# Query and key projection with high and low parts side by side, and ScalarE writing 40 pairs of convolution tap products

## The reference, cut to what matters

```python
h = rmsnorm(x, pre_norm_g) * (1.0 + scale) + shift
proj = h @ w_in
q, k, v, z_ret, u_val, u_gate, z_conv, g_a, g_b = split(proj)
qh = rotary(q); kh = rotary(k) * 256 ** -0.5             # 4 heads of 256
ret = head_groupnorm(retention_chunkwise(qh, kh, v))
y_a = (ret * silu(z_ret)) @ w_ret_out
a = u_val * sigmoid(u_gate)
a = causal_depthwise_conv_2(a, conv_w, conv_b)           # 31 taps, 1024 channels
a = silu(layernorm(a, conv_ln_g, conv_ln_b))
y_b = (a * silu(z_conv)) @ w_conv_out
y = (sigmoid(g_a) * y_a + sigmoid(g_b) * y_b) @ w_out
```

## Time and profile before

| | |
|---|---|
| median of 3 runs | 837.8 us (837.55 to 839.03) |
| the profiled execution | 837.87 us, of which the span of the trace is 836.1 us |
| TensorE busy | 827.8 us, 99% |
| VectorE busy | 731.1 us, 87% |
| ScalarE busy | 500.2 us, 60% |
| granted TensorE clock | 0.999 of full speed |

### The profile page before, as it was taken

The page is one execution under the profiler, slowest core; times in us unless marked ns, Lnnn a source line. Parts: engine busy times, 40 slices in busy tenths (PEclk is TensorE's granted clock), DMA queues, the critical chain, the costliest instruction groups (busy, mean ns, idle before and its releaser), DMA issues.

```text
span 836.1 us, 13942 instructions
## 1 busy us (share of the span) xinstructions
PE 827.8 (99%) x5146; PEld 725.1 (87%) x5146; DVE 731.1 (87%) x1179; ACT 500.2 (60%) x804; POOL 45.4 (5%) x46
## 2 busy tenths in 40 slices
PE   8999999999999999999999999999999999999997
PEld 8999998789888888888888788998887798888886
DVE  7799899868877898888989979999999999988774
ACT  6899858576566555555565775333346675546743
POOL 0001101341100000000000000000001220000000
PEclk9999999999999999999999999999999999999999
DMA  9875675511875877777776656655454435564531
GB/s 277 256 253 169 211 245 174 146 38 45 278 232 179 261 262 263 257 256 252 238 257 218 221 185 213 202 184 169 155 198 151 152 118 200 186 231 171 188 115 50
DMA packets 129882, 164.13 MB, mean 196 GB/s; under 512 B 17407, under 2 KB 92199, under 8 KB 129703
## 3 DMA queue, kind: packets, MB, share of 16 engines
q1 hardware_dynamic: 129831, 163.45, 59.9%
HBM read 159.20 MB, written 4.23 MB: 195 GB/s over the span
## 4 chain that ended last, share of the span: by engine, by line
PE 98%; DVE 1%; DMA 1%; issue 0%; ACT 0%; DVEq 0%; SPq 0%; ACTq 0%
PE psum L695 16%; PE psum L727 14%; PE psum L728 14%; PE psum L734 14%; PE psum L704 8%; PE psum L677 6%; PE psum L686 6%; PE psum L678 6%; PE psum L1028 2%; PE psum L631 1%; PE psum L641 1%; PE psum L635 1%; PE psum L1033 1%; PE psum L915 1%; PE psum L1146 1%; PE psum L1134 1%
## 5 line engine op out<-in xcount | busy, mean ns | idle before, releaser
L1220 ACT ACTIVATE w_hi<-w_raw 128x1024 fp32r<-128x1024 f32 x255 | 266.6, 1061 | 188.2 <-PE psum L734 87.1
L1786 DVE TENSOR_TENSOR w_lo<-w_raw,w_hi 128x1024 fp32r<-128x1024 f32 x256 | 305.2, 1221 | 44.3 <-ACT w_hi L1220 42.2
L695 PE MATMUL psum<-hT,w_hi 128*128 128x512 f32 x576 | 138.9, 391 | 0.0
L695 PEld LDWEIGHTS psum<-hT,w_hi 128*128 128x128 f32 x576 | 105.4, 188 | 20.2
L727 PE MATMUL psum<-w_hi,hT 128*128 128x512 f32 x280 | 113.3, 405 | 0.0
L728 PE MATMUL psum<-w_hi,hT 128*128 128x512 f32 x280 | 109.3, 390 | 0.0
L2399 DVE SCALAR_TENSOR_TENSOR cv<-aP,par,cv 128x256 f32<-128x256 f32 x240 | 107.9, 519 | 0.0
L677 PE MATMUL psum<-hT,w_hi 128*128 128x256 f32 x432 | 107.4, 286 | 0.0
L678 PE MATMUL psum<-hT,w_hi 128*128 128x256 f32 x432 | 105.9, 283 | 0.0
L677 PEld LDWEIGHTS psum<-hT,w_hi 128*128 128x128 f32 x432 | 82.8, 192 | 0.4 <-issue 0.2
L678 PEld LDWEIGHTS psum<-hT,w_hi 128*128 128x128 f32 x432 | 82.9, 192 | 0.3 <-issue 0.2
(11 more groups left out here) (341 smaller groups left out, 1108.6 us busy)
## 6 DMA issues: line engine op xcount, KB each, us to landing
w_raw<-in_w_in_dram SPq DMA_DIRECT2D x44, 1024.0 KB, 5.1
w_raw<-in_sc_w_in_dram SPq DMA_DIRECT2D x32, 1024.0 KB, 7.9
w_raw<-in_gdn_w_in_dram SPq DMA_DIRECT2D x23, 1024.0 KB, 7.1
ada<-in_w_ada_dram SPq DMA_DIRECT2D x24, 512.0 KB, 4.8
w_raw<-in_gdn_w_out_dram SPq DMA_DIRECT2D x8, 1024.0 KB, 5.5
w_raw<-in_sc_w_out_dram SPq DMA_DIRECT2D x8, 1024.0 KB, 6.4
w_raw<-in_w_ret_out_dram SPq DMA_DIRECT2D x8, 1024.0 KB, 5.1
w_raw<-in_w_conv_out_dram SPq DMA_DIRECT2D x4, 1024.0 KB, 5.1
```

The lines of the kernel that those rows point to most:

```text
L695: pe.matmul(o, w_hi[s][:, k, mine], hT[:, h * KH2 + k, :, :], start=h == 0 and k == 0, stop=False, skip_group_check=True)
L1220: act.activation((w_hi[half_slot(g, h)] if home is None else third_hi[half_slot(g, home)])[:, :, :], raw[slot][:, h * KH2:(h + 1) * KH2, : ...
L1786: return dve.tensor_tensor(o, whole, hi.bitcast(F32), ALU.subtract)
```

## The change

TensorE: qk uses `chunk_apart`, still in a hardware loop, and the scores of v's chunk 0 wait for a doubled count of `rp_step`. ScalarE: in each step of qk it copies the low parts' share from PSUM to SBUF (`glu_part`). In qk, v and zret it also writes products of a window and a tap's weight for a pair of channel blocks (`make_taps`, two ACTIVATE of 128 x 256 for each of the 40 pairs), ahead of the phase's own work; there are two buffers at a time, so that each pair waits for the addition of the one before the last. VectorE: `rotate` first adds the two shares (`ug_sum`) and multiplies that sum; of the convolution 80 operations L2399 go and 40 additions of 128 x 512 come. The shares are now 1 addition in each chunk of qk, 4 operations and 2 additions in each of v and zret (chunk 2 of zret, where a pair of blocks ends, has 6 and 2), 8, 5, 5, 5 in zconv, 6, then five times 10, then 1 in gates. Each operation waits by `tap_before` for the last one on its own block. Waits of other engines on `cv_step` follow the new counts, and ScalarE's phases qk and v are unrolled.

```diff
+CONV_SHARES = [("glu", [(0, 0), (0, 0), (3, 0), (4, 0), (5, 0), (4, 0), (2, 0), (4, 0)]), ("qk", [(0, 1)] * 8), ("v", [(4, 2)] * 8),
+               ("zret", [(4, 2)] * 8), ("zconv", [(8, 0), (5, 0), (5, 0), (5, 0)]), ("gates", [(6, 0)] + [(10, 0)] * 7)]
+TAP_PHASES = ("qk", "v", "zret")
+
+
+def conv_order():
+    order, ends, part = [], [], {}
+    pair, tap, e = 0, 0, 0
+    for name, counts in CONV_SHARES:
+        for c, (singles, made) in enumerate(counts):
+            mine = part[name, c] = []
+            while (singles or made) and pair < KT // 2:
+                if singles or e or tap == 0:
+                    mine.append(("one", pair, tap, e))
+                    tap, e, singles = tap + e, 1 - e, max(singles - 1, 0)
+                else:
+                    mine.append(("made", pair, tap, None))
+                    tap, made = tap + 1, made - 1
+                order.append(mine[-1])
+                if tap == CW:
+                    ends.append(len(order))
+                    pair, tap = pair + 1, 0
+    assert pair == KT // 2
+    return order, ends, part
...
+def tap_before(i):
+    kind, pair, tap, e = CONV[i]
+    return max(j for j in range(i) if CONV[j][1] == pair and (e is None or CONV[j][3] in (None, e))) + 1
...
+        made = [at(f"made{s}", o_yT + 2 * s * K, [P, 2, SEQ]) for s in range(2)] + [at(f"made{s}", o_ada + 2 * (s - 2) * K, [P, 2, SEQ]) for s in (2, 3)]
+
+        def made_in(k):
+            first = sum(len([entry for entry in CONV_PART[name, c] if entry[0] == "made"])
+                        for name, cs in (("qk", range(COUNT["qk"])), ("v", range(4))) for c in cs)
+            return made[k % 2 + 2 * (k >= first)]
...
-                        elif name in ("sc_in", "glu"):
+                        elif name in ("sc_in", "glu", "qk"):
...
-                    pe.wait_ge(rp_step, 2 * RH)
+                    pe.wait_ge(rp_step, 4 * RH)
...
+            def make_taps(name, c):
+                for entry in CONV_PART[name, c]:
+                    kind, pair, tap, _ = entry
+                    if kind != "made":
+                        continue
+                    k = MADE.index(entry)
+                    act.wait_ge(bank_free, 4 + FIRST["qk"])
+                    if k >= 2:
+                        act.wait_ge(cv_step, CONV.index(MADE[k - 2]) + 1)
+                    if made_in(k) is not made[0] and made_in(k) is not made[1]:
+                        act.wait_ge(st_ready, RH)
+                    for e in range(2):
+                        n = 2 * pair + e
+                        w = par[:, 2 + tap // 16, tap % 16 * KT + n:tap % 16 * KT + n + 1]
+                        i = act.activation(made_in(k)[:, e, :], aP[:, n, tap:tap + SEQ], ACT.Copy, scale=w)
+                    i.then_inc(tap_made, 1)
...
-            chunks("qk")
+
+            def beside_qk_2(i, j, done):
+                c, g = 4 * i + j, FIRST["qk"]
+                make_taps("qk", c)
+                act.wait_ge(half_done, done)
+                act.wait_ge(bank_free, 4 + g + c - 1)
+                act.activation(glu_part[j % 2][:, :, :], psum[:, 2 * j:2 * j + 2, SEQ:2 * SEQ], ACT.Copy).then_inc(sc_act, 1)
+            chunks("qk", beside_qk_2, unroll=True)
...
-            chunks("v", tokens_out(vt, ACT.Copy))
+            v_out = tokens_out(vt, ACT.Copy)
+
+            def beside_v(i, j, done):
+                make_taps("v", 4 * i + j)
+                v_out(i, j, done)
+            chunks("v", beside_v, unroll=True)
...
+                make_taps("zret", c)
...
+                if kind == "made":
+                    k = MADE.index(CONV[i])
+                    dve.wait_ge(tap_made, k + 1)
+                    dve.tensor_tensor(cv[:, both, :], cv[:, both, :], made_in(k)[:, :, :], ALU.add).then_inc(cv_step, 1)
+                    return
...
-                    dve.wait_ge(cv_step, step - 1)
...
-                conv_share(3)
+                conv_share("qk", c)
                 dve.wait_ge(half_done, done)
-                dve.tensor_tensor(rp1[:, :, :], bank(j), cos2, ALU.mult)
-                dve.tensor_tensor(rp2[:, :, :], bank(j), sin2, ALU.mult).then_inc(bank_free, 1)
+                dve.wait_ge(sc_act, 6 * KT - 2 + COUNT["glu"] - 2 + c + 1)
+                dve.tensor_tensor(ug_sum[:, :, :], psum[:, 2 * j:2 * j + 2, 0:SEQ], glu_part[j % 2][:, :, :], ALU.add).then_inc(bank_free, 1)
                 dve.wait_ge(bank_free, 4 + FIRST["qk"] + c + 1)
+                dve.tensor_tensor(rp1[:, :, :], ug_sum[:, :, :], cos2, ALU.mult)
+                dve.tensor_tensor(rp2[:, :, :], ug_sum[:, :, :], sin2, ALU.mult).then_inc(rp_step, 1)
+                dve.wait_ge(rp_step, 2 * c + 1)
                 dve.tensor_tensor(qkT[:, 2 * c:2 * c + 1, :], rp1[:, 0:1, :], rp2[:, 1:2, :], ALU.subtract)
                 dve.tensor_tensor(qkT[:, 2 * c + 1:2 * c + 2, :], rp2[:, 0:1, :], rp1[:, 1:2, :], ALU.add).then_inc(rp_step, 1)
-                dve.wait_ge(rp_step, c + 1)
+                dve.wait_ge(rp_step, 2 * c + 2)
...
-                conv_share(9 if c < RH else 8)
+                conv_share("v", c)
...
-                conv_share(7)
+                conv_share("zret", n)
...
-                conv_share(5 if j else 8)
+                conv_share("zconv", j)
...
-                conv_share(10 if c else 4)
+                conv_share("gates", c)
```

More of the change, by code:

```diff
@@ L93 @@
 SHIFTED = ((4, 5, 6, 7), (6, 7))
+CONV_SHARES = [("glu", [(0, 0), (0, 0), (3, 0), (4, 0), (5, 0), (4, 0), (2, 0), (4, 0)]), ("qk", [(0, 1)] * 8), ("v", [(4, 2)] * 8),
[20 more added lines that the diff above has]
+    return order, ends, part
+CONV, CONV_ENDS, CONV_PART = conv_order()
+MADE = [entry for entry in CONV if entry[0] == "made"]
+def tap_before(i):
+    kind, pair, tap, e = CONV[i]
+    return max(j for j in range(i) if CONV[j][1] == pair and (e is None or CONV[j][3] in (None, e))) + 1
 E_LEAST = 0.5 * math.log(RMS_EPS) - 0.1
@@ L281, in build @@
         ba_hi_ready, ba_lo_ready, ba_done = sem("ba_hi_ready"), sem("ba_lo_ready"), sem("ba_done")
-        beta_ready, gate_v, gate_a, g_ready = (
-            sem(n) for n in ("beta_ready", "gate_v", "gate_a", "g_ready"))
+        tap_made, gate_v, gate_a, g_ready = (
+            sem(n) for n in ("tap_made", "gate_v", "gate_a", "g_ready"))
         bg_turned, bgt_ready, eg_ready = sem("bg_turned"), sem("bgt_ready"), sem("eg_ready")
@@ L1468, in _ @@
                     act.wait_ge(cleared, 1)
-                    act.activation(bg[0:VH, :], psum[0:VH, 6, 0:SEQ], ACT.Sigmoid).then_inc(beta_ready, 1)
+                    act.activation(bg[0:VH, :], psum[0:VH, 6, 0:SEQ], ACT.Sigmoid)
                     act.activation(acols[gr, 2:3], acols[gr, 0:1], ACT.Exp).then_inc(gate_a, 1)
@@ L1775, in _ @@
             pool.wait_ge(rg_ready, NT * RH)
-            pool.wait_ge(cv_step, CW * 4)
+            pool.wait_ge(cv_step, CONV_ENDS[1])
             pool.tensor_tensor(ln_sum[0][:, :, :], cv[:, 0:2, :], cv[:, 2:4, :], ALU.add).then_inc(ln_sum_step, 1)
             pool.wait_ge(ln_sum_step, 1)
-            pool.wait_ge(cv_step, CW * 6)
+            pool.wait_ge(cv_step, CONV_ENDS[2])
             pool.tensor_tensor(ln_sum[0][:, :, :], ln_sum[0][:, :, :], cv[:, 4:6, :], ALU.add).then_inc(ln_sum_step, 1)
@@ L2387, in _, with conv_op @@
             dve.memset(aP[:, :, 0:CPAD], 0.0).then_inc(padded, 1)
-            def conv_op(pair, tap, e):
-                n, step = 2 * pair + e, 2 * CW * pair + 2 * tap + e
+            conv_done = [0]
+            def conv_op(i):
+                kind, pair, tap, e = CONV[i]
+                both = slice(2 * pair, 2 * pair + 2)
+                if tap == 0 and e == 0:
+                    dve.wait_ge(bank_free, 4 + FIRST["glu"] + 2 * pair + 2)
+                if tap:
+                    dve.wait_ge(cv_step, tap_before(i))
+                if kind == "made":
[3 more added lines that the diff above has]
+                    return
+                n = 2 * pair + e
                 w = par[:, 2 + tap // 16, tap % 16 * KT + n:tap % 16 * KT + n + 1]
                 src = aP[:, n, tap:tap + SEQ]
-                if tap == 0 and e == 0:
-                    dve.wait_ge(bank_free, 4 + FIRST["glu"] + 2 * pair + 2)
                 if tap == 0:
@@ L2397, in conv_op, with conv_share @@
                 else:
-                    dve.wait_ge(cv_step, step - 1)
                     dve.scalar_tensor_tensor(out=cv[:, n, :], in0=src, scalar=w, in1=cv[:, n, :], op0=ALU.mult, op1=ALU.add).then_inc(cv_step, 1)
[L2401 to L2405, removed]
+            def conv_share(name, c):
+                for entry in CONV_PART[name, c]:
+                    conv_op(conv_done[0])
+                    conv_done[0] += 1
             def glu_each(i, j, done):
@@ L2427, in glu_each @@
                 if c >= 2:
-                    conv_share((3, 4, 5, 4, 2, 4)[c - 2])
+                    conv_share("glu", c)
                 if c == 6:
@@ L2509, in last_pairs @@
                 c = 4 * i + j
```

(6 more changed lines are left out.)

## The result

The changed kernel takes 839.83 us (median of 8 runs, 839.71 to 840.98) against 837.48 us of the kernel before in the same series (8 runs): ratio 1.0027, 95% interval 1.0016 to 1.0038. It is slower by 2.35 us. The forecast was 839.9, within 837.0 to 841.8, and slower. The profiled execution has a span of 837.9 us against 836.1.

The account below looks back on a forecast made before the run. TensorE, busy 99% of the span, was taken to bound the kernel. The form's -1.6, the scores' +0.3 and 3.4 us of waits gave +2.1, from 837.8 to 839.9 us, range 837.0 to 841.8.

Parts of the forecast that it names:

- TensorE's form: In qk, a chunk on TensorE falls from 5.76 to 5.56 us in the apart form; eight chunks give -1.6 us.
- The scores: At v's chunk 0, TensorE asks at 571.7 but the last rotation is done at 572.0: +0.3 us.
- Price of the taps on VectorE: In v and zret, a share of four operations and two additions takes 3.02 us; zret gets 0.25 a chunk heavier.
- rival B: VectorE's waits cost nothing beyond 0.60 us between starts, zret's share is 2.78: +0.9, 838.7 us; chance 0.15.
- The taps ahead of the root: In zret's chunk 2, two pairs of taps on ScalarE delay the group norm's square root, so VectorE starts 1.6 us later.
- Rival D: ScalarE is early enough that taps are not in the root's way, rest as forecast: +0.5, 838.3 us; chance 0.1.
- Lateness against cushions: VectorE 3.6 us late against 2.05 at zconv, 4.4 against 1.0 at gates' chunk 7: 3.4 us of TensorE waits.
- waits of about 0.8 us in each of chunks 5 to 7: Sign in gates: TensorE waits at w_lo products, since VectorE's step takes 6.24 us and TensorE's 5.47 at most.
- The sum: Whole kernel: -1.6 + 0.3 + 3.4 = +2.1 us, median from 837.8 to 839.9, 0.25% up.
- Rival A: Lateness at gates' chunk 7 stays under 1.0 us, no w_lo is late: 836.2 to 836.5 us; chance 0.12.
- rival C: Lateness also reaches other waits, such as zconv's transposes or w_hi: +4, 841.8 us; chance 0.13.

Follow-up runs that it names:

- all_three: Changed kernel with zret's taps behind the group norm, eight operations moved from zret to v, qk's rotation before the tap addition: 835.99 us, 0.998 of before.

## Why the prediction was right

*TensorE's form, -1.6 us.* Eight chunks of 3.65 + 1.91. TensorE was 0.31 us ahead at the start of qk and 1.16 at zconv, after 0.7 lost at the scores, so the form gave 1.55. `all_three` shows it alone: 306.63 - 305.06 = 1.57.

*The scores, +0.3.* The step on VectorE was 5.72 us, as summed; the last rotation was waited for 0.46 us. With what the matmuls around a wait lose (the scores took 1.57 us instead of 1.31) it came to 0.70. The term was right in place and too small, by 0.16 us in the wait and by 0.24 in that loss, which I had left out of all waits.

*Price of the taps on VectorE.* 3.04 us a share against 3.02 forecast and 2.78 of rival B, which falls by this. The Trainium skill ("VectorE: DVE Perf Modes", section "The DRAIN you can't avoid") measured no cost of semaphores between chained operations of VectorE. The trace differs: 0.72 us from start to start with a wait and 0.61 without, in one step of qk.

*The taps ahead of the root, +1.6 us of lateness.* VectorE's idle time rose by 1.60, and undoing it gave 1.53 us. Rival D falls.

*Lateness against cushions, +3.4.* At zconv 3.6 us as summed; TensorE lost 1.76 (forecast 1.55). At gates the term was mis-sized: I had 4.4 us of lateness, it was 3.6 (VectorE's w_lo 2.47 us later, 740.34 against 737.87, and TensorE 1.16 ahead if it had not waited), and the loss in gates was 1.25 us where 1.8 was forecast. I had announced waits of about 0.8 us in each of chunks 5 to 7. The trace lists one, of 0.50 us in chunk 7; chunk 6 lost about 0.3 us without a wait in the list, chunk 5 nothing. The two operations more in gates' chunk 0 did cost 0.8, but as much came back in zconv, in a place that I had taken as unchanged. Before, GpSimd's second sum fell on two operations of VectorE on SBUF tiles and held them up; now it starts at another point of VectorE's order, beside the low parts that read PSUM, and holds up only a w_lo behind them, by 0.2 us. GpSimd and VectorE before, then GpSimd and VectorE in the changed kernel:

```profile
694.84 1.33 POOL L1780 TENSOR_TENSOR ln_sum<-ln_sum,cv 128x512 f32<-128x512 f32 x1 [11.33 <-DVE cv L2399]
```

```profile
694.61 1.71 DVE L2396 TENSOR_SCALAR cv<-aP,par 128x256 f32<-128x256 f32 x2
```

```profile
698.07 1.30 POOL L1852 TENSOR_TENSOR ln_sum<-ln_sum,cv 128x512 f32<-128x512 f32 x1 [12.11 <-DVE cv L2481]
```

```profile
697.84 1.28 DVE L1858 TENSOR_TENSOR yT_lo<-psum,yT_hi 128x512 fp32r<-128x512 f32 x2
699.04 2.54 DVE L1858 TENSOR_TENSOR w_lo<-w_raw,w_hi 128x1024 fp32r<-128x1024 f32 x2
701.51 0.72 DVE L2479 TENSOR_SCALAR cv<-aP,par 128x256 f32<-128x256 f32 x2
```

The pair of TENSOR_SCALAR takes 1.71 us in one and 0.72 in the other. No run moves GpSimd's sum alone; the account rests on these overlaps in time.

*The sum.* Forecast -1.6 + 0.3 + 3.4 = +2.1; in the traces -1.55 + 0.70 + 1.76 + 1.25 = +2.16. The agreement within 0.1 us is partly luck: the scores and zconv were 0.6 too low together, gates 0.55 too high. Rival A (cushions hold) did not happen in the changed kernel; it is what `all_three` makes of it. Of rival C, the wait for w_hi in zconv (0.24 us) is there in small; no transpose waited.

## What to carry to other kernels

Work taken off a busy engine counts only behind the last point at which that engine had caught up, and against the cushion of each buffer there: here VectorE's total stayed the same, and 3.7 us were lost at TensorE, which had run without a gap. Four waits of 0.2 to 1.1 us make 2.3 of them; the rest went in the products around the waits. Before moving work to a less busy engine, look at what that engine answers next and who waits for the answer; put the moved work behind it. And leave the lighter share where the consumer's step is shortest: moving eight operations to chunks with the scores gave 2.5 us of the changed kernel's loss back, with no work saved.

## What the hardware showed that was not expected

The clock: after one wait of TensorE of 3.85 us, behind two small ones of 0.23 and 0.53, the granted clock was 0.50 to 0.52 for 3 us and cost some 1.4 us (scores 2.93 us against 1.57 behind a wait of 1.97 us, where the clock stayed at 1.00). Each is one profiled execution. The waits of 0.46 and 1.97 us cost only themselves and some 0.25 us in the scores behind them; those of 0.24 and 1.12 us in zconv cost 1.76 together.

GpSimd did not hold up every operation of VectorE: beside a GpSimd addition two low parts with an operand in PSUM kept their 1.28 us for the pair, while a pair of operations on SBUF alone was held until it had ended (1.71 us instead of 0.72). The w_lo behind the low parts is the same kind of operation with both operands in SBUF; GpSimd's last 0.33 us (to 699.37) fell on it, and it took 0.2 us longer (2.54 against 2.34). So it seems to be the place of the operands that counts; no run was made to test it.
